# Unused buffers of 16 to 640 bytes placed ahead of weight or activation buffers in five dense stages

## The reference

```
h = rmsnorm(x);  z = h @ w_in                      # 1024 -> 3328: q, k, v, u_ssm, two gates
y_attn = windowed_gqa(q, k, v) @ w_branch_attn     # |t-s| <= 128, ALiBi, sink, 8 heads of 64
y_ssm  = glu(gelu(s5_bidirectional(u)), w_glu) @ w_branch_ssm
merged = sigmoid(gate_a) * y_attn + sigmoid(gate_s) * y_ssm
x = x + rmsnorm(merged @ w_out)
h2 = rmsnorm(x)
f = gelu(dwconv3(h2 @ w_ffn_gate) + b) * (h2 @ w_ffn_up)    # 1024 -> 2816, twice
return x + rmsnorm(f @ w_ffn_down)                 # 2816 -> 1024
```

## The kernel before

| stage | stationary, starts at | moving, starts at | stationary minus moving, modulo 512 |
|---|---|---|---|
| pi | w_hi 187136 | feat_hi 32896 | 128 |
| br | w_hi 20608 | attn_hi 28800, y_hi 127104 | 0 |
| ou | g_hi 139488 | w_hi 65760 | 0 |
| gu | w_hi 187136 | feat_hi 16512 | 128 |
| dn | f_hi 150752 | w_hi 49376 | 0 |

## Time and profile before

### The profile page before, as it was taken

One profiled execution on the slowest core, in us unless ns is written; L12 is line 12 of the kernel. 1 busy time (PEld: TensorE's weight loads), 2 busy tenths in 40 slices (PEclk: granted clock), 3 DMA queues, 4 the chain that ended last, 5 costly groups with the idle time before them and its releaser, 6 DMA issues. The chain is left out here.

```text
span 3358.3 us, 36601 instructions
## 1 busy us (share of the span) xinstructions
PE 3083.7 (92%) x13014; PEld 2449.0 (73%) x13014; DVE 1165.1 (35%) x1396; ACT 714.1 (21%) x1160; POOL 486.7 (14%) x829
## 2 busy tenths in 40 slices
PE   6699999947999998799894999999999997999998
PEld 5588888735666666587684788888888886788886
DVE  5000000086757550644333422222222222322433
ACT  4011111114333331500212211111111111212321
POOL 1530000083876000000111000000000000000111
PEclk9899999968555558899897999999999999999999
DMA  3322122133110105433644211111111111634563
GB/s 119 76 75 75 61 70 75 53 63 45 33 33 22 33 24 85 176 150 133 192 138 130 64 44 50 50 50 35 46 50 50 50 44 55 191 92 122 169 171 120
DMA packets 298293, 278.18 MB, mean 83 GB/s; under 512 B 46336, under 2 KB 269824, under 8 KB 288512
## 3 DMA queue, kind: packets, MB, share of 16 engines
q1 hardware_dynamic: 253536, 160.94, 17.4%
q0 software_dynamic: 13248, 68.16, 5.6%
q10 hardware_dynamic: 31456, 48.42, 4.7%
HBM read 191.50 MB, written 83.89 MB: 82 GB/s over the span
## 5 line engine op out<-in xcount | busy, mean ns | idle before, releaser
L325 PE MATMUL gu_banks<-gu_feat_hi,gu_w_hi 128*128 128x512 f32 (+1 forms) x1408 | 557.2, 396 | 1.0 <-DVE gu_feat_lo L235 1.0
L326 PE MATMUL gu_banks<-gu_feat_hi,gu_w_lo 128*128 128x512 f32 (+1 forms) x1408 | 556.0, 395 | 0.0
L327 PE MATMUL gu_banks<-gu_feat_lo,gu_w_hi 128*128 128x512 f32 (+1 forms) x1408 | 555.8, 395 | 0.0
L325 PE MATMUL pi_banks<-pi_feat_hi,pi_w_hi 128*128 128x512 f32 (+1 forms) x832 | 331.4, 398 | 30.5 <-DVE pi_w_lo L317 29.5
L326 PE MATMUL pi_banks<-pi_feat_hi,pi_w_lo 128*128 128x512 f32 (+1 forms) x832 | 329.8, 396 | 0.0
L327 PE MATMUL pi_banks<-pi_feat_lo,pi_w_hi 128*128 128x512 f32 (+1 forms) x832 | 329.7, 396 | 0.0
L325 PEld LDWEIGHTS gu_banks<-gu_feat_hi,gu_w_hi 128*128 128x128 f32 x1408 | 265.8, 189 | 62.9 <-DVE gu_feat_lo L235 1.4
L327 PEld LDWEIGHTS gu_banks<-gu_feat_lo,gu_w_hi 128*128 128x128 f32 x1408 | 265.5, 189 | 61.9
L326 PEld LDWEIGHTS gu_banks<-gu_feat_hi,gu_w_lo 128*128 128x128 f32 x1408 | 265.7, 189 | 61.4
L325 PE MATMUL dn_y<-dn_w_hi,dn_f_hi 128*128 128x512 f32 x704 | 276.5, 393 | 23.8 <-DVE dn_w_lo L799 23.8
L326 PE MATMUL dn_y<-dn_w_hi,dn_f_lo 128*128 128x512 f32 x704 | 275.6, 391 | 0.0
(11 more groups left out here) (236 smaller groups left out, 4339.3 us busy)
## 6 DMA issues: line engine op xcount, KB each, us to landing
dn_f_raw<-f SPq DMA_DIRECT2D x64, 704.0 KB, 5.9
f<-gu_conv POOLq DMA_DIRECT2D x22, 1024.0 KB, 4.1
gates<-pi_rows_out ACTq DMA_DIRECT2D x16, 1024.0 KB, 4.3
br_rows<-gates POOLq DMA_DIRECT2D x16, 1024.0 KB, 6.9
pi_w_raw<-in_w_in SPq DMA_DIRECT2D x26, 512.0 KB, 4.7
gu_w_raw<-in_w_ffn_gate SPq DMA_DIRECT2D x22, 512.0 KB, 3.7
gu_w_raw<-in_w_ffn_up SPq DMA_DIRECT2D x22, 512.0 KB, 3.7
dn_w_raw<-in_w_ffn_down POOLq DMA_DIRECT2D x22, 512.0 KB, 6.7
```

Of the source, the lines that this page charges most:

```text
L325: pe.matmul(out, w_hi, x_hi, start=first, stop=False)
L326: pe.matmul(out, w_lo, x_hi, start=False, stop=False)
L327: return pe.matmul(out, w_hi, x_lo, start=False, stop=last)
```

## The change

One line is added to each of five stages: an allocation of a buffer called `shift` that nothing writes or reads. It moves every buffer that is allocated behind it.

```
 in stage_project_in                 bases.enter(m, nt.normed[:]...)
+        m.sb("shift", [P, 96])
                                     ws = WeightStream(m, KD)
 in stage_gate_up                    nt = NormTranspose(m, x_mid, gain)
+        m.sb("shift", [P, 160])
                                     ws = WeightStream(m, KD)
 in stage_down                       w_lo = m.sb("w_lo", [P, KF, BANK], F32R)
+        m.sb("shift", [P, 32])
                                     f_raw = m.sb("f_raw", [P, 2, KH, P])
 in stage_branches                   ws = WeightStream(m, K)
+        m.sb("shift", [P, 16])
                                     attn_hi = m.sb("attn_hi", [P, K, TOK], F32R)
 in stage_out                        w_lo = m.sb("w_lo", [P, KD, D], F32R)
+        m.sb("shift", [P, 4])
                                     g_raw = m.sb("g_raw", [P, 2, KD, P])
```

## The result

The changed kernel takes 3342.14 us (median of 3 runs, 3341.76 to 3344.08), the kernel before 3361.35; the ratio is 0.9942, 95% interval 0.9919 to 0.9965. Forecast was 3340. The profiled execution took 3344.08 us, with a span of 3342.5 against 3358.3.

A forecast was written before the change was run, and what follows sets the result against it. TensorE's matmul stream bounds the dense stages, so time is count times pace. Terms of -16 (pi), -24 (gu), +13 (dn) and +6 (br, ou) sum to -21 us from 3361.35: 3340 us, range 3325 to 3371.

The forecast's parts named there:

- the sorting of the stages: Dense stages: stationary minus moving start modulo 512 is 128 in slow pi and gu, 0 in quick br, ou, dn.
- two paces: Time per matmul before the change: 233.4 ns in pi and 232.4 in gu, 226.6 in br, ou and dn.
- a table of addresses: Start addresses of the stationary and moving operands in each dense stage, from which their differences were taken.
- -16 and -24 forecast: pi and gu: difference leaves 128 for 0 and 256, so both reach 226.6 ns, saving 16 and 24 us.
- The open choice: gu: no row showed a difference of 256; bounds 0 to 24.1 us saved, taken as quick like 0, 24 us.
- +13 forecast: dn: difference goes from 0 to 128, so it gets pi's or gu's pace and loses 11.9 to 13.9 us.
- +3.2 forecast: br: difference goes from 0 to 448, loss of 0 to 6.4 us, half taken.
- +2.6 forecast: ou: difference goes from 0 to 32, loss of 0 to 5.1 us, half taken.
- its bound of 5.1: ou: largest loss in us, if its 757 matmuls at full pace ran at the slow 233.4 ns.
- the sum's -28 to -15: All five dense stages: range of the summed change in us, with dn, br and ou at their extremes.
- The sum of -21: All five dense stages: -16 - 24 + 13 + 6 us, taken from the median of 3361.35.
- Addresses don't matter: Rival, pi and gu: the two paces come from something else and stay, 3361 us (3359 to 3366); chance 0.22.

The follow-up runs named there:

- Experiments 1 to 3: The kernel before with other pads, as all_zero, both_moved and The map: 3323.36 us, 3323.4 us, and 3390.04, 3380.47 and 3383.75 us.
- all_zero: Kernel before plus one 128-byte shift ahead of the weights in pi and gu only, difference 0 modulo 256 in all five stages: 3323.36 us, ratio 0.9895.
- both_moved: all_zero plus a pad ahead of all of each stage's buffers, moving both operands by 32 to 160 bytes, difference still 0: 3323.4 us, one run.
- The map: Three kernels: the kernel before with one pad per stage, sized for differences modulo 256 from 32 to 224: 3390.04, 3380.47 and 3383.75 us.
- experiment 5: all_zero with finer differences, 16 bytes in pi and br, 8 in gu, 4 in ou, 240 in dn: 3359.59 us, one run.

## Why the prediction was right

The step that carried it was the sorting of the stages: it took only two paces, a table of addresses and the exclusion of code, of other engines' load and of chance. Experiments 1 to 3 show it to be the cause: same instructions, other addresses, and each stage goes where its difference says.

- `pi` and `gu`, -16 and -24 forecast, -15.3 and -23.5 measured. The open choice, that 256 is as good as 0, held, and `all_zero` and `both_moved` show it again in `pi`.
- `dn`, +13 forecast, +11.5 measured. It took `gu`'s pace of 232.4 rather than `pi`'s 233.4, the lower end of the term. Why `pi` alone has 233.3 at 128 isn't known.
- `br`, +3.2 forecast, +2.1 measured; `ou`, +2.6 forecast, +5.8 measured. Here the reasoning was wrong though the sum wasn't hurt: I took a difference between 0 and 128 to give a pace between. The map shows that 32, the nearest to 0, is as slow as 128 or slower, 96 is the slowest and 192 a narrow good place. The duration in `ou` came out at 395 and not between. Of the sum of these two, 6, it measured 7.9, and `ou`'s 5.8 lies beyond its bound of 5.1; its pace alone gives 757 x 6.6 = 5.0. That the two halves came near together is luck: with 32 in `br` too, its 936 matmuls would have lost 6.2 in place of 2.1, and the dense stages would have saved some 15 us, an estimate at the far end of the sum's -28 to -15.
- The sum of -21 stands against -19.4 for the dense stages and -19.2 between the medians. The last two agree better than they have to: the two profiled spans differ by only 15.8.
- "Addresses don't matter" was right in its detail that one difference allows several paces (experiment 5, and `pi`'s 232.6 and 233.4 before), wrong in the main. The Trainium skill's page "SBUF — State Buffer" says in "Who interferes with whom" that TensorE and ScalarE never wait on anyone. That is about other engines and no run here speaks against it. The Trainium skill's page "TensorE: Matmul & The Clock Gate" says in "Step-by-step: what each phase is for" that the next weights' load takes no read bandwidth from the running matmul. What the prediction drew from it, that the places of the two operands can't matter, doesn't hold here: mean durations go from 388 to 399 ns by these places, at one clock, with loads of 188 ns. Whether read bandwidth is what is lost no run here shows.

What is shown is the dependence on the two places, and not on either alone. That the weight load and the moving stream meet in a shared part of SBUF would be one explanation; no run here shows it.

## What to carry to other kernels

When dense stages with one matmul shape and one granted clock show different durations, put the operands' start addresses beside them, before looking for a cause in the code. For fp32r blocks of 128 x 128 against 128 x 512, each with its own weight load, start both operands at one residue modulo 256 bytes, in all pairs that a stage uses, low parts too; here that made the slow stages 2.4 to 2.9% shorter per matmul and the kernel 1.05% for two lines. Any new buffer ahead of one of them can undo it. No other shape or format was tried.

## What the runs showed of the hardware

- The pace of such a stream at 2.4 GHz lies from 226.7 to 234.3 ns with the difference, and repeats after 256 bytes at the six differences met in both halves of 512. It isn't monotonic; from starts it is 226.7, 233.3, 233.3, 234.3, 232.4 or 233.3, 233.3, 228.9, 233.3 for 0, 32, ... 224.
- Four bytes are enough to leave the quick pace (`ou` at 4: 232.5 ns, one run). At 16 bytes both 226.7 and 233.4 ns were seen, within one stage.
- The low clock hides it: in the changed kernel the first matmuls of `br` run at the lower level, 1.2 GHz (granted clock 0.50 from 1342 to 1345 us), with 0.43 us from start to start, as in the earlier trace rows, though the difference is 192 there and was 0 before. The same 0.43 us stands behind a gap in all five stages of these two traces, at differences of 0, 32, 128 and 192.

```profile
1342.71 0.63 PE L327 MATMUL br_banks<-br_y_lo,br_w_hi 128*128 128x512 f32 x1
1343.14 0.63 PE L325 MATMUL br_banks<-br_y_hi,br_w_hi 128*128 128x512 f32 x1
1343.56 0.63 PE L326 MATMUL br_banks<-br_y_hi,br_w_lo 128*128 128x512 f32 x1
1343.99 0.63 PE L327 MATMUL br_banks<-br_y_lo,br_w_hi 128*128 128x512 f32 x1
```
